# Token chunks of 384, 384 and 304, norms spread into the groups ahead of them, and seven blocks joined into three, in an encoder step on one core

## The reference

```python
def ffn_step(h, g, b, wg, wu, wd):
    return layer_norm(ALPHA * h + 0.5 * swiglu(h, wg, wu, wd), g, b)
h = ffn_step(h, ln1_g, ln1_b, ffn1_wg, ffn1_wu, ffn1_wd)
(q, k, v, qi, ki, wi), rec, gates = mixer_inputs(h, w_in, lb)
oa = attend(q, qi, wi, k, v, ki)
orec, S = recur(*rec)
mixed = (sigmoid(ga) * (oa @ wa) + sigmoid(gb) * (ob @ wb)) @ wo
h = layer_norm(ALPHA * h + mixed, ln2_g, ln2_b)
y = ffn_step(h, ln3_g, ln3_b, ffn2_wg, ffn2_wu, ffn2_wd)
```

## Time and profile before

| | |
|---|---|
| median of 3 runs | 2971.89 us (2968.10 to 2976.58) |
| profiled execution, span | 2966.0 us; no other time of it is given |
| PE busy | 2739.8 us, 92%, 16384 matmuls |
| DVE busy | 1378.5 us, 46% |
| ACT busy | 632.2 us, 21% |
| POOL busy | 513.7 us, 17% |
| DMA | 149.13 MB, 50 GB/s over the span |

### The profile page before, as it was taken

How to read it: one execution, slowest core, us unless ns; L and a number is a source line. 1 busy time by engine, 2 the same in 40 slices (tenths; PEclk the granted TensorE clock), 3 DMA queues, 4 the chain that set the end, 5 groups by cost and what they waited for, 6 DMA issues and landing times. The chain is left out here.

```text
span 2966.0 us, 41425 instructions
## 1 busy us (share of the span) xinstructions
PE 2739.8 (92%) x16384; PEld 2638.8 (89%) x16384; DVE 1378.5 (46%) x2882; ACT 632.2 (21%) x1081; POOL 513.7 (17%) x183
## 2 busy tenths in 40 slices
PE   6999999999978999999869986799799999999995
PEld 6999999999957899999759975799599999999995
DVE  1333333333356689993075526666553333333336
ACT  3111111111023622122245533210311111111102
POOL 1211111122012012112100002121221112222112
PEclk9999999999988999999858987799999999999997
DMA  3111111111022011222200000422211111111101
GB/s 130 53 48 42 42 42 42 42 42 42 1 60 63 22 36 43 95 88 95 89 15 31 1 1 8 154 67 73 71 43 43 42 42 42 42 50 49 42 0 73
DMA packets 134941, 149.13 MB, mean 50 GB/s; under 512 B 19072, under 2 KB 119520, under 8 KB 134704
## 3 DMA queue, kind: packets, MB, share of 16 engines
q1 hardware_dynamic: 131376, 134.45, 14.4%
q10 hardware_dynamic: 3456, 13.17, 1.1%
HBM read 123.82 MB, written 23.79 MB: 50 GB/s over the span
## 5 line engine op out<-in xcount | busy, mean ns | idle before, releaser
L485 DVE TENSOR_TENSOR ffn_prod<-ffn_gate,ffn_psu 128x358 f32<-128x358 f32 x132 | 69.6, 527 | 808.3 <-ACT ffn_gate L373 808.3
L65 PE MATMUL ffn_psg<-h_hi,ffn_up_hi 128*128 128x358 f32 (+1 forms) x1056 | 345.4, 327 | 23.8 <-DVE h_lo L262 12.5
L65 PE MATMUL ixp_ps<-h_hi,ixp_hi 128*128 128x358 f32 (+1 forms) x1032 | 338.7, 328 | 24.3 <-issue 17.3
L65 PE MATMUL ffn_psd<-ffn_hid_hi,ffn_dn_hi 128*128 128x358 f32 (+1 forms) x1056 | 346.6, 328 | 11.4 <-DVE y L504 10.4
L504 DVE TENSOR_TENSOR y<-y,ffn_psd 128x358 f32<-128x358 f32 (+1 forms) x480 | 251.0, 526 | 209.4 <-PE ffn_psd L67 209.4
L66 PE MATMUL ffn_psg<-h_lo,ffn_up_hi 128*128 128x358 f32 (+1 forms) x1056 | 346.1, 328 | 0.0
L67 PE MATMUL ffn_psg<-h_hi,ffn_up_lo 128*128 128x358 f32 (+1 forms) x1056 | 345.5, 327 | 0.0
L373 ACT ACTIVATE ffn_gate<-ffn_psg 128x358 f32<-128x358 f32 x132 | 62.0, 470 | 1329.7 <-PE ffn_psu L67 1329.7
L66 PE MATMUL ffn_psd<-ffn_hid_lo,ffn_dn_hi 128*128 128x358 f32 (+1 forms) x1056 | 344.5, 326 | 0.0
L66 PE MATMUL ffn_psu<-h_lo,ffn_up_hi 128*128 128x358 f32 (+1 forms) x1056 | 344.3, 326 | 0.0
L67 PE MATMUL ffn_psd<-ffn_hid_hi,ffn_dn_lo 128*128 128x358 f32 (+1 forms) x1056 | 344.3, 326 | 0.0
(11 more groups left out here) (289 smaller groups left out, 4936.2 us busy)
## 6 DMA issues: line engine op xcount, KB each, us to landing
ffn_dn_raw<-in_ffn_wd SPq DMA_DIRECT2D x22, 1024.0 KB, 4.9
ixp_raw<-in_w_in SPq DMA_DIRECT2D x39, 512.0 KB, 3.8
spill<-y ACTq DMA_DIRECT2D x24, 536.0 KB, 2.7
up_raw<-in_ffn_wg SPq DMA_DIRECT2D x11, 1024.0 KB, 5.4
up_raw<-in_ffn_wu SPq DMA_DIRECT2D x11, 1024.0 KB, 7.9
ffn_up_raw<-in_ffn_wg SPq DMA_DIRECT2D x11, 1024.0 KB, 5.4
ffn_up_raw<-in_ffn_wu SPq DMA_DIRECT2D x11, 1024.0 KB, 7.9
mo_sig<-spill SPq DMA_DIRECT2D x16, 536.0 KB, 4.7
```

The source lines that it names most:

```text
L65: pe.matmul(out, w_hi, x_hi, start=first, stop=False)
L485: dve.tensor_tensor(prod[:, k % 2, 0:w], gate[:, k % 2, 0:w], ps_up[k % 3][:, 0:w], ALU.mult).then_inc(prod_done, 1)
```

## The change

`CHUNKS` becomes 384, 384 and 304 tokens. Every SBUF tensor gets an address written out by hand instead of coming from a stack of allocations, which lets phases overlap in place. Phases 1, 2 and 3 share one block (`front`, with `index_and_project` behind it in the same block), `mixers` keeps its own with its code unchanged, and phases 5, 6 and 7 share another (`back`). Within these:

- Loading: nine slots instead of three; the first up weights come in two halves of 128 columns, one after three token tiles and one after six; PE transposes three tiles, starts the first up, and turns the other tiles between the ups. The rest of these first weights is made by DVE, and `h_lo` is made from `y` in SBUF.
- The last group of each feed-forward part goes chunk by chunk with two banks for gates and two for ups, the other pair being free for the next norm or the next transposes. The middle groups 1 to 9 keep their instructions.
- The first layer norm runs inside the last group of the first part and the first index products; four index tiles are buffered ahead instead of two.
- The mixer output goes by pairs of tiles and by chunks: downs of a chunk follow the ups of the next one. The last pair has two output banks instead of four and takes in mean and variance of chunk 0 and the mean of chunk 1; the norm's other steps stand in the first group of the second feed-forward part. SP loads the gates of the second tile without a wait, then `y`, the norm's constants and the first up weights.
- The last norm's transposes run inside the last group; its rows are multiplied and shifted in place in four buffers.

```diff
-CHUNKS = [(0, 358), (358, 358), (716, 356)]
+CHUNKS = [(0, 384), (384, 384), (768, 304)]
...
+def front(c, block, dram, st):
...
+        for j in range(2):
+            for t in range(3 * j, 3 * j + 3):
+                ld.load(sp, t)
+            f.load_up_first(sp, j)
...
+        f.pe_middle(pe)
+        f.up_last(pe, 0)
+        f.up_last(pe, 1)
+        f.up_last(pe, 2)
+        f.down_last(pe, 0)
+        f.up_last(pe, 3)
+        pe.wait_ge(f.y_done, 24 * L + 8)
+        norm.mean(pe, 0)
+        f.down_last(pe, 1)
+        f.up_last(pe, 4)
+        norm.variance(pe, 0)
+        f.up_last(pe, 5)
+        pe.wait_ge(f.y_done, 24 * L + 16)
+        norm.mean(pe, 1)
+        f.down_last(pe, 2)
...
+        for t in range(3):
+            ld.copies(act, t)
+        f.split_up(act, 0, 0, "none")
...
+            ld.rests(dve, t)
+        f.rest_up(dve, 0, 0)
...
+        f.sums_last(dve, 1)
+        norm.centre(dve, 0)
+        f.hidden_last(dve, 4)
+        norm.scale_shift(dve, 0)
+        f.hidden_last(dve, 5)
+        f.sums_last(dve, 2)
...
+def index_and_project(c, block, dram, st, f, norm):
...
+        norm.ready(pe, 0)
+        pe.wait_ge(f.prod_done, 6 * GROUPS)
+        pr.multiply(pe, 0, 0)
+        norm.variance(pe, 1)
+        pr.multiply(pe, 1, 0)
+        pe.wait_ge(f.y_done, 24 * GROUPS)
+        norm.mean(pe, 2)
+        pr.multiply(pe, 2, 0)
+        pr.multiply(pe, 3, 0)
+        norm.variance(pe, 2)
+        for i in (1, 2):
+            norm.ready(pe, i)
+            for n in range(pr.FIRST):
+                pr.multiply(pe, n, i)
...
+def back(c, block, dram, st):
...
+        norm.squares(act, 0)
+
+        act.wait_ge(mul_done, 6 * KD)
+        f.split_up(act, 0, 0, "none")
+        f.split_up(act, 0, 1, "none")
+        norm.deviation(act, 0)
+        norm.heads(act, 0)
...
+        pool.wait_ge(up_mm, 3 * KD)
+        f.rest_up(pool, 0, 0)
+        f.rest_up(pool, 0, 1)
+        for n in range(3):
+            norm.first_rests(pool, n)
...
+        for i in range(PAIRS):
+            for x in range(3):
+                up(i, x)
+            down(i, 0)
+            up(i, 3)
+            if i == PAIRS - 1:
+                pe.wait_ge(y_done, 24 * i + 8)
+                norm.mean(pe, 0)
+                up(i, 4)
+                down(i, 1)
+                up(i, 5)
+                norm.variance(pe, 0)
+                pe.wait_ge(y_done, 24 * i + 16)
+                norm.mean(pe, 1)
+            else:
+                up(i, 4)
+                down(i, 1)
+                up(i, 5)
+            down(i, 2)
+        pe.wait_ge(y_done, 24 * PAIRS)
+        norm.mean(pe, 2)
+        for x, j, n in f.BY_CHUNK:
+            if j == 0:
+                norm.ready(pe, n)
...
+            mix(i, 5)
+            if i == PAIRS - 1:
+                norm.scale_shift(dve, 0)
+            sums(i, 2)
+        norm.centre(dve, 1)
+        norm.centre(dve, 2)
+        f.hidden(dve, 0, 0, 0, 0, first=True)
+        norm.scale_shift(dve, 1)
...
+        for t in range(2, 5):
+            ln.turn(pe, t)
+        f.down_last(pe, 2)
+        for t in range(5, ln.NT):
+            ln.turn(pe, t)
```

More of the change, by code:

```diff
@@ L107, in store_rows @@
     return 48
[L110 to L156, removed]
@@ new lines, in index_and_project, with scores @@
+    h_out = [sem(f"h_out{i}") for i in range(3)]
+    units = []
+    for b in list(range(1, NB)) + ["s"]:
+        for h in range(HEADS):
+            units += [(b, h, k0, w) for k0, w in pieces(SCORE_AT[b][1])]
+    EARLY = 9
+    gap = len(units) // EARLY
+    early = {gap * (j + 1) - 1: (NI + j // 3, j % 3) for j in range(EARLY)}
+    index = {x[:3]: n for n, x in enumerate(units)}
+    blocks = [(n, b, QB) for n, b in enumerate(range(1, NB))] + [(NB - 1, "s", DEC)]
+    def scores(b, rows):
+        at, keys = SCORE_AT[b]
+        return c.score[0:rows, at:at + keys]
@@ new lines, in _ @@
+    @block.sync
+    def _(sp):
+        norm.load(sp, dram)
+        sp.wait_ge(f.up_lo_done, 2 * GROUPS)
+        pr.load(sp, 0)
+        pr.load(sp, 1)
+        for half in range(2):
+            sp.dma_start(kidx_rows[:, :, half * DH:(half + 1) * DH],
+                         dram["cache_kidx"].rearrange("(n p) d -> p n d", p=P)).then_inc(kidx_in, 16)
+        pr.load(sp, 2)
+        pr.load(sp, 3)
+        for n in range(3):
+            t0, w = CHUNKS[n]
+            sp.wait_ge(norm.shifted, KD * (n + 1))
+            sp.dma_start(c.y_spill[:, :, t0:t0 + w], c.y[:, :, t0:t0 + w]).then_inc(h_out[n], 16)
+        for n in range(4, NI + 3):
+            pr.load(sp, n)
+        sp.wait_ge(ki_done, len(TT))
+        n_out = store_rows(sp, ki_tok, dram["new_kidx_p"], dram["new_kidx_s"], ki_out)
+        for n in range(NI + 3, NTL):
+            pr.load(sp, n)
+        sp.wait_ge(ki_out, n_out)
@@ new lines, in back @@
+    dn_hi, dn_lo = at(177920, "dn_hi", [P, 2, KD, P], F32R), at(177920 + 8192, "dn_lo", [P, 2, KD, P], F32R)
+    sig = [[at(o, f"sig{t}{g}", [P, T]) for g, o in enumerate(os)]
+           for t, os in enumerate(((c.UP_HI, c.UP_HI + 4288), (c.UP_HI + 8576, c.DN_HI + 12288)))]
+    pa, pb = at(c.GATE, "pa", [P, CW]), at(c.GATE + 1536, "pb", [P, CW])
+    with ExitStack() as own:
+        ps = [[c.ps(own, f"mo_ps{n}{i}", [P, 512]) for i in range(2)] for n in "ab"]
+        ps_dn = [c.ps(own, f"mo_psd{i}", [P, 512]) for i in range(4)]
@@ new lines, in _, with split_up, split_down @@
+    @block.scalar
+    def _(act):
+        def split_up(t):
+            act.wait_ge(up_in, 32 * (t + 1))
+            if t >= 2:
+                act.wait_ge(up_mm, 6 * (t // 2) - 1 + t % 2)
+            act.activation(up_hi[:, t % 2], up_raw[:], ACT.Copy).then_inc(up_hi_done, 1)
+        def split_down(t):
+            act.wait_ge(dn_in, 16 * (t + 1))
+            if t == 0:
+                act.wait_ge(x_lo_done, 6)
+            if t >= 2:
+                act.wait_ge(dn_mm, 24 * (t // 2))
+            act.activation(dn_hi[:, t % 2], dn_raw[:], ACT.Copy).then_inc(dn_hi_done, 1)
+        for n, (t0, w) in enumerate(CHUNKS):
+            for g in range(2):
+                act.activation(x_hi[:, g, :, t0:t0 + w], outs[g][:, :, t0:t0 + w], ACT.Copy).then_inc(x_hi_done, 1)
+            if n == 0:
+                split_up(0)
+        split_up(1)
+        for t in range(0, KD, 2):
+            split_down(t)
+            split_down(t + 1)
+            if t + 2 < KD:
+                split_up(t + 2)
+                split_up(t + 3)
+        norm.squares(act, 0)
+        act.wait_ge(mul_done, 6 * KD)
+        f.split_up(act, 0, 0, "none")
+        f.split_up(act, 0, 1, "none")
+        norm.deviation(act, 0)
+        norm.heads(act, 0)
+        norm.squares(act, 1)
+        f.silu(act, 0, 0, 0, first=True)
+        norm.deviation(act, 1)
+        norm.squares(act, 2)
+        f.silu(act, 0, 1, 0, first=True)
+        norm.heads(act, 1)
+        norm.deviation(act, 2)
+        f.silu(act, 0, 2, 1, first=True)
+        norm.heads(act, 2)
+        for k in range(3, 6):
+            if k == 3:
+                f.split_down(act, 0, True)
+            if k == 5:
+                f.split_up(act, 1, 0, "chunk")
+            f.silu(act, 0, k, f.BY_CHUNK[k][2], first=True)
+        f.act_middle(act)
+        f.split_up(act, L, 1, "tile")
+        f.split_down(act, L)
+        for k in range(4):
+            f.silu(act, L, k, f.BY_CHUNK[k][2], 2)
+        ln.deviation(act, 0)
+        ln.normalise(act, 0)
+        f.silu(act, L, 4, 2, 2)
+        ln.deviation(act, 1)
+        ln.normalise(act, 1)
+        f.silu(act, L, 5, 2, 2)
+        ln.deviation(act, 2)
+        for s in range(3, ln.NT + 1):
+            ln.act_step(act, s)
```

1773 lines of the change are left out of this document (944 added, 829 removed).

## The result

The changed kernel takes 2981.53 us (median of 6 runs, 2976.26 to 2986.97) against 2970.26 for the kernel before (6 runs): a ratio of 1.0041, 95% interval 1.0026 to 1.0056. It is slower by 0.4%, where 2962 was forecast, 0.3% faster, in a range of 2932 to 2986 that takes the measured time in. The profiled execution has a time of 2977.88 and a span of 2976.2 us, 10.2 more than the span of before.

A forecast was written before the change was run, and what follows sets the result against it. PE was taken as hardly ever idle in long stretches, with idle time in the seams. Terms -16.5 - 6 - 2.5 + 22 - 6.5 = -9.5 against the 2966.0 span gave 2956.5; with 5.9 for the median, 2962 us, range 2932 to 2986.

The forecast's parts named there:

- Front: Start to first down: first up needs only three token tiles and half the weights; -16.5 us, from -18 to -12.
- Chunk widths: Feed-forward groups: a narrower last chunk shortens PE's wait for sums in 20 middle and last groups; -6 us, -10.4 to 0.
- First join: Between first feed-forward part and score units: stalls of about 32 us against 35.4 before; -2.5 us, from -10 to +5.
- Score units, projections, mixers: The stretch from first score unit through the mixers: unchanged, 0 us.
- Back: Mixer output to first down of second feed-forward part: new waits in the pairs; +22 us, from +8 to +30.
- Last pair of the back: Last mixer-output pair: stalls of 17 to 20 us replace 18.6, plus some 4 of slow clock, less 1; +5.1 us.
- Tail: Last group to end: work moved ahead gives two tiles' lead, 7.3 us less 0.8; -6.5 us, from -9 to -2.
- A: Rival: chain waits in the joins vanish; first join -6, back +5, total -30, 2942 us; chance .25.
- B: Rival: after the last pair's long stall TensorE stays at 1.2 GHz through 50 to 95 us; about 2998 us; chance .17.
- its sign of over 35 us at 0.50 in back: Sign that the forecast is wrong by the clock rival: granted clock of 0.50 for over 35 us in the back.
- C: Rival: parts don't do what they say; front only -8, chunk widths 0; +5 in sum, 2977 us, no change; chance .13.
- the signs that the forecast named for being right: First up near 18, downs near 73, group wait 0.2, last-pair wait 10 to 13, `y` wait near 25, end 6 to 7 shorter.

The follow-up runs named there:

- the run with the filler: Changed kernel plus 24 matmuls of 384 columns, results not used, ahead of down 2 in each of the first three pairs; 2971.87 us in one run.
- the run with POOL held back: Changed kernel with POOL's rests of the next pair's two up weights waiting until DVE ended the gate steps of ups 4 and 5; 2968.79 us in one run.

## Why the prediction was wrong

The sign was wrong: -9.5 us against the span was forecast, +10.2 came. The difference of 19.7 is the sum over the table of what came less what was forecast:

- **Front**, right: -16.7 against -16.5; first up at 17.53 against 17.9, downs at 72.80 against 73.
- **Chunk widths**, right in mechanism, a little large: -5.0 against -6; the run with the old widths gives 2.3 and 2.6 back. A group's wait for the sums is 0.26 in the middle groups where 0.2 was said.
- **First join**, the step that failed first: +5.8 against -2.5. The forecast gave `scale_shift` 3.1 to 5.13 us for its eight scale-and-shifts and took them as DVE's alone. They took 10.39, as the first index weights' rests of POOL fall on them in the new order, and the wait ahead of the last down was 13.48 in place of 6 to 8. Held back, the join is 199.0, within the forecast's range. The other waits of the join came as listed.
- **Score units, projections, mixers**: -6.2 against 0, of which 2.2 are the chunk widths in the first two and the rest scatter. It hides a part of what the other terms cost.
- **Back**, the step that failed most: +37.5 against +22. The excess of 15.5 lies in pairs 0 to 2. Their lengths grew by 17.1, 7.3 and 8.7, where 12.5, 2.2 and 2.2 were forecast. From the table of pairs, PE's idle time there grew by 12.1, 5.7 and 5.9 us (11.5, 2.2 and 2.2 forecast) and its busy time for the same matmuls by 5.0, 1.5 and 2.8 (1, 0 and 0 forecast). So two terms were too small. One is the wait of down 2 for up 5's five gate steps, given as 1.3 to 4 us: it was 4.44 to 4.82. POOL's rest of the next weights, which ACT starts when up 5 is done, falls on the same steps and adds 2.0, and a second rest falls on the steps of up 4 and adds 0.80 in down 1. The other is the low clock behind the short waits, 8.4 us more than forecast in these pairs; the run with the filler shows for three of the waits that the dip comes with PE's idleness.
- **Last pair of the back**: +4.5 against +5.1, in part by luck. The long chain and its blocked products were worked out well: 14.43 us in down 2 against 13, 7.10 against 7. But PE's idle time grew by 5.7 us where some 1 was forecast, as the two large waits were 21.5 us in place of 17 to 20 and small ones of 2.7 us came to them, and its busy time fell by 1.2 where 4 us of slow clock were added: the kernel before had its own low clock there, behind waits of 2.98 and 12.48. The two errors cancel.
- **Tail**, near: -5.3 against -6.5. No run tests the lead of two tiles from which it was worked out.

Two sums of the prediction do not come out as written. Its terms for the last pair (17 to 20, less 18.6, plus 4, less 1) give 1.4 to 4.4, not 5.1, and its terms for the front 16.3, not 16.5. Neither changes the sign.

The forecast had priced POOL's hold on DVE in one place, +3 in the last pair, and had the row that shows it. It did not ask it of the other places where the change puts a POOL rest beside DVE steps on PE's path. A second sign of it lay in its own bounds for the join: the 5.13 us of the earlier trace rows ran from 852.37 to 857.50 beside this rest of POOL in the kernel before, and the same eight steps take 3.10 without one (run with the old widths).

```profile
852.11 2.55 POOL L685 TENSOR_TENSOR ixp_lo<-ixp_raw,ixp_hi 128x1024 fp32r<-128x1024 f32 x1 [4.78 <-ACT ixp_hi L681]
```

The Trainium skill's rule of an exclusive port pair ("SBUF — State Buffer", section "SBUF: two separate sides") is what these runs show for an add with two inputs in SBUF (2.52 against 0.47 us). The scale-and-shifts (10.39 against 3.20) read one tensor from SBUF; the rule also counts VectorE's steps in a mode that uses both ports, and no run here shows in which mode these were.

Of the rivals, A (the joins hide) is refuted by the waits. B (the clock stays low for 50 to 95 us) has the time on its side, and its sign of over 35 us at 0.50 in back came true in sum: the mean clocks of the two rows of back make some 44 us at the lower level, against some 22 before. But it came in eight pieces, and none was the long stay that B is about: after the wait of 14.43 us the granted clock was 0.58 in the next 4.6 us and 1.00 behind that. The cost was the 8.1 us of longer busy time and not 25 to 47. C did not come either: the parts did what they say, and the waits outweighed them.

Nearly all the signs that the forecast named for being right came true: the first up and the downs, the wait for the sums in a group, the long wait in the last pair, a wait for `y` some 29 us after the mixers. None of them looked at the join or at pairs 1 and 2, where the forecast failed.

## What to carry to other kernels

When work is spread into another engine's stream, list for each step of the new chain what POOL does in the same microseconds, not only what stands ahead of it in its own queue. In an interleaved order put a second independent product between a product and the one that needs its element-wise steps: here the same products in another order were worth 23 us, a part of it because POOL's rest then fell on other steps. A short wait can cost more than its length: here matmuls at half speed followed most waits of 4 us and more.

## What the runs showed of the hardware

Short waits of PE were followed by a dip of the granted clock: 0.50 to 0.61 in the 4 us behind the three waits of 4.4 to 4.8. Of the waits of 2.4 to 2.8 us in the run with POOL held back, two had a dip and one had none. Matmuls that only kept PE busy in a wait took the dip away. An add of two tensors in SBUF by DVE took 2.52 us beside POOL's subtraction and 0.47 without, a cast 2.34 against 0.32, while a sum with one operand in PSUM took 0.55 beside it. Eight scale-and-shifts of 384 columns by DVE, with one tensor read, took 3.2 times as long beside POOL's subtractions as without them.
